# A mixture-of-experts phase in which row indices are listed four blocks ahead and rows gathered three blocks ahead

## The reference

```
scores = sigmoid(xt @ router_w);  sel = scores + router_bias
idx    = top 8 of sel within the best 4 of 8 groups;  wts = scores[idx] / sum * 2.5
# the (token, expert) pairs are sorted by expert and padded to blocks of 128 slots, one expert each
h  = silu(xb @ w1[e]) * (xb @ w3[e])        # xb: 128 gathered rows, w1, w3: 1024 x 256
yb = h @ w2[e]                              # w2: 256 x 1024
out[token] += yb * weight;  out += shared expert
```

## Time and profile before

| | us |
|---|---|
| median of 3 runs | 3874.74 |
| lowest and highest | 3873.43 and 3879.52 |
| span of the profiled execution | 3881.8 |
| from the start of the first scatter to that of the last, layer 0 | 1154.1 to 2146.9 |
| the same, layer 1 | 2901.8 to 3843.6 |

### The profile page before, as it was taken

The page is one execution under the profiler, slowest core; times in us unless marked ns, Lnnn a source line. Parts: engine busy times, 40 slices in busy tenths (PEclk is TensorE's granted clock), DMA queues, the critical chain, the costliest instruction groups (busy, mean ns, idle before and its releaser), DMA issues. The chain is left out here.

```text
span 3881.8 us, 56399 instructions
## 1 busy us (share of the span) xinstructions
PE 3178.2 (82%) x12323; PEld 2159.6 (56%) x12324; DVE 2164.1 (56%) x3866; ACT 1584.7 (41%) x2332; POOL 501.2 (13%) x606
## 2 busy tenths in 40 slices
PE   7988999997768888888888399888668788888884
PEld 1144667763446666666666144454336666666663
DVE  1253433334357767767667520584357777777575
ACT  0033222222136555556555311343135665665564
POOL 0000000000002222222222000000002222222221
PEclk9988555568778898999998699899678988888996
DMA  8721000002059989888888410100348898999796
GB/s 313 251 92 46 1 1 0 1 1 103 37 191 305 301 248 300 289 264 263 255 252 267 161 65 0 46 1 1 118 173 281 286 304 288 300 302 304 226 290 187
DMA packets 156081, 690.47 MB, mean 178 GB/s; under 512 B 15036, under 2 KB 22844, under 8 KB 105044
## 3 DMA queue, kind: packets, MB, share of 16 engines
q1 hardware_dynamic: 111368, 526.73, 36.3%
q0 software_dynamic: 43776, 159.40, 17.7%
q10 hardware_dynamic: 848, 3.24, 0.2%
HBM read 596.95 MB, written 92.37 MB: 178 GB/s over the span
## 5 line engine op out<-in xcount | busy, mean ns | idle before, releaser
L1628 DVE TENSOR_TENSOR e_w13l<-ring,e_w13h x512 | 593.0, 1220 | 67.5 <-issue 44.1
L1536 ACT CAST e_w13h<-ring x512 | 498.1, 1044 | 152.9 <-issue 93.4
L1454 PE MATMUL e_psH<-e_w13h,e_xh 128*128 x1184 | 467.4, 395 | 4.5 <-ACT e_xh L1556 4.0
L1454 PE MATMUL e_psH<-e_w13l,e_xh 128*128 x1184 | 464.1, 392 | 0.0
L1439 PE MATMUL e_psT<-m_id,e_xg 128*128 128x128 f32 x1200 | 209.6, 329 | 260.3 <-DMA e_xg<-h_rows,e_gidx 260.0
L1478 PE MATMUL e_psY<-e_w2h,e_gh 128*128 128x512 f32 x592 | 317.3, 536 | 84.4 <-DVE e_w2l L1615 74.9
L453 PE MATMUL psP<-ring,ho 128*128 128x512 f32 x800 | 350.9, 594 | 0.0
L1393 POOL DMA_INDIRECT y_rows<-e_y,e_sidx x148 | 290.3, 1961 | 369.1 <-ACT e_y L1564 193.8
L1439 PEld LDWEIGHTS e_psT<-m_id,e_xg 128*128 128x128 f32 x1200 | 174.3, 202 | 280.1 <-issue 263.7
L1615 DVE TENSOR_TENSOR e_w2l<-ring,e_w2h 128x1024 fp32r<-128x1024 f32 x256 | 301.2, 1217 | 27.3 <-ACT e_w2h L1525 19.9
L1556 ACT CAST e_xh<-e_psT 128x512 fp32r<-128x512 f32 x300 | 166.5, 588 | 315.3 <-PE e_psT L1439 312.9
(11 more groups left out here) (259 smaller groups left out, 4402.1 us busy)
## 6 DMA issues: line engine op xcount, KB each, us to landing
ring<-in_exp_w SPq DMA_DIRECT2D x388, 1024.0 KB, 5.4
ring<-in_ada_w SPq DMA_DIRECT2D x24, 2048.0 KB, 8.4
ring<-in_c_w_in SPq DMA_DIRECT2D x6, 2048.0 KB, 14.4
bc<-mod_rows SPq DMA_DIRECT2D x4, 1536.0 KB, 8.2
r_bc<-mod_rows SPq DMA_DIRECT2D x4, 1536.0 KB
ring<-in_sh_w SPq DMA_DIRECT2D x6, 1024.0 KB
h_rows<-r_hrow SPq DMA_DIRECT2D x10, 512.0 KB, 2.9
y_rows<-r_y SPq DMA_DIRECT2D x10, 512.0 KB, 2.6
```

The costliest lines, as they stand in the source:

```text
L1454: nc.tensor.matmul(psH[par][:], xh[par][:, k * P:(k + 1) * P], w[:, bass.DynSlice(half, 1), :, k, :], start=(k == 0 and i == 0), stop=False)
L1536: nc.scalar.copy(w13h[:, bass.DynSlice(half, 1), :, k, :].rearrange("p o u k n -> p (o u) (k n)"), raw13[:, bass.DynSlice(half, 1), :, k, ...
L1628: nc.vector.tensor_tensor(low, raw, high.bitcast(F32), ALU.subtract).then_inc(w13_lo, 1)
```

## The change

In experts:

- The row numbers and weights of all blocks go into columns of two tables, e_idxs and e_gws, one column a block. POOL copies a column to e_gidx before a gather and to e_sidx before a scatter; the weight is read by ACT straight from its column.
- choose runs five blocks ahead, index and indices four ahead of the block whose gate is transposed (index(b + 4) and indices(b + 3) in step b), and the gather of b + 5 is issued ahead of scatter(b + 1), so rows are gathered about three blocks ahead. There are still two buffers xg.
- The spare rows move behind the real ones, and an empty slot's row number is T + p (T tokens, p the partition). The gather has a bound: row numbers above T are skipped, and the buffer keeps what was there. xg is cleared once at the start. The scatter still writes all 128 rows.
- PE's order in a step is hidden(b), turn(b + 1), turn_gate(b), index(b + 4), down(b - 1).
- ACT computes SiLU in one instruction instead of the sigmoid, and DVE multiplies once instead of twice.
- ACT's order is silu(b), rows_in(b + 1), gate(b), two of the four pieces of w1 and w3 for b + 2, rows_out(b - 1), split2(b), the other two pieces. DVE's is product(b), indices(b + 3), rows_in(b + 1), gate(b), two pieces, choose(b + 5), rest2(b), the other two pieces.
- The gathers of two blocks behind the last one are gone.

The diff, cut to its core (the starts and ends of the loops and the declarations are left out in part):

```diff
-                link(nc.vector.memset(r.tab5[:, i, :, 3], float((i + 1) * P)))
+                link(nc.vector.memset(r.tab5[:, i, :, 3], float(i * P - T - P)))
             link(nc.vector.tensor_copy(r.tab5[:, :, :, 4], part[:, 0:1].unsqueeze(2).to_broadcast([P, n_t, E])))
-            link(nc.vector.tensor_copy(r.spare[:], part[:, 0:1]))
+            link(nc.vector.tensor_scalar(r.spare[:], part[:, 0:1], float(T), None, ALU.add))
...
+            link(nc.vector.tensor_scalar(r.table[0:1, last + 5:last + 6], r.table[0:1, last + 2:last + 3], 2.0, -4.0, ALU.mult, ALU.add))
...
             def gather(b, par):
-                pool.wait_ge(idx_ready, b + 1)
                 wait_for(pool, xt_mm, 2 * (b - 1))
                 pool.sem_inc(pool_clear, 1)
-                nc.gpsimd.indirect_dma_start(xg[par][:], None, s.hrows[l], bass.IndirectOffsetOnAxis(ap=gidx[par][:, 0:1], axis=0)
-                                             ).then_inc(gathered[par], 16)
+                pool.wait_ge(idx_ready, b + 1)
+                nc.gpsimd.tensor_copy(gidx[par][:], idxs[:, at_block(b)]).then_inc(g_copied, 1)
+                pool.wait_ge(g_copied, b + 1)
+                pool.sem_inc(pool_clear, 1)
+                nc.gpsimd.indirect_dma_start(xg[par][:], None, s.hrows[l], bass.IndirectOffsetOnAxis(ap=gidx[par][:, 0:1], axis=0),
+                                             bounds_check=T, oob_is_err=False).then_inc(gathered[par], 16)
             def scatter(b, par):
-                if isinstance(b, int) and b < 0:
-                    return
-                pool.wait_ge(copied, 2 * b + 2)
+                wait_for(pool, added, 16 * b)
+                pool.sem_inc(pool_clear, 1)
+                nc.gpsimd.tensor_copy(sidx[par][:], idxs[:, at_block(b)]).then_inc(s_copied, 1)
                 pool.wait_ge(y_ready, b + 1)
-                wait_for(pool, added, 16 * b)
+                pool.sem_inc(pool_clear, 1)
+                pool.wait_ge(s_copied, b + 1)
                 pool.sem_inc(pool_clear, 1)
                 nc.gpsimd.indirect_dma_start(s.yrows[l], bass.IndirectOffsetOnAxis(ap=sidx[par][:, 0:1], axis=0), ysb[par][:], None,
                                              compute_op=ALU.add).then_inc(added, 16)
-            def keep(b, par):
-                wait_for(pool, added, 16 * (b - 1))
-                pool.sem_inc(pool_clear, 1)
-                nc.gpsimd.tensor_copy(sidx[par][:], gidx[par][:]).then_inc(copied, 1)
-                nc.gpsimd.tensor_copy(sw[par][:], gw[par][:]).then_inc(copied, 1)
-            def step(b, par):
-                keep(b, par)
-                gather(b + 2, par)
-                scatter(b - 1, 1 - par)
             n = pairs(pool)
+            for par in range(2):
+                nc.gpsimd.memset(xg[par][:], 0.0).then_inc(xg_clean, 1)
+            pool.wait_ge(xg_clean, 2)
...
+            scatter(0, 0)
+            with pool.Fori(0, n - 2) as i:
+                gather(2 * i + 5, 1)
+                scatter(2 * i + 1, 1)
+                gather(2 * i + 6, 0)
+                scatter(2 * i + 2, 0)
...
+            def step(b, m, par):
+                hidden(b, par)
+                turn(b + 1, m, 1 - par)
+                turn_gate(b)
+                index(b + 4, par)
...
-            def pair(i):
-                hidden(2 * i + 1, 1)
-                index(2 * i + 3, 1)
-                turn_gate(2 * i)
-                turn(2 * i + 2, i + 1, 0)
-                down(2 * i, 0)
...
+            step(0, 0, 0)
+            step(1, 1, 1)
+            down(0, 0)
+            with pe.Fori(0, n - 1) as i:
+                step(2 * i + 2, i + 1, 0)
                 down(2 * i + 1, 1)
-            pair(0)
-            with pe.Fori(0, n - 1) as i:
-                pair(i + 1)
-            turn_gate(2 * n)
-            down(2 * n, 0)
+                step(2 * i + 3, i + 2, 1)
+                down(2 * i + 2, 0)
...
-            def expo(b, par):
+            def silu(b, par):
                 act.wait_ge(h_mm, b + 1)
-                wait_for(act, g_step, b)
-                nc.scalar.activation(ge[:], psH[par][:, 0:F], ACT.Sigmoid).then_inc(e_ready, 1)
+                wait_for(act, g_ready, b)
+                nc.scalar.activation(ge[:], psH[par][:, 0:F], ACT.Silu).then_inc(e_ready, 1)
...
-                act.wait_ge(copied, 2 * b + 2)
                 wait_for(act, added, 16 * (b - 1))
-                nc.scalar.activation(ysb[par][:], psY[:], ACT.Copy, scale=sw[par][:, 0:1]).then_inc(y_ready, 1)
+                nc.scalar.activation(ysb[par][:], psY[:], ACT.Copy, scale=gws[:, at_block(b)]).then_inc(y_ready, 1)
             def step(b, par):
-                expo(b, par)
-                gate(b - 1, 1 - par)
+                silu(b, par)
                 rows_in(b + 1, 1 - par)
-                split13(b + 2, range(PIECE))
-                rows_out(b - 1, 1 - par)
+                gate(b, par)
+                split13(b + 2, range(2))
+                if not isinstance(b, int) or b > 0:
+                    rows_out(b - 1, 1 - par)
                 split2(b)
+                split13(b + 2, range(2, PIECE))
...
-            def indices(b, par):
+            def indices(b):
                 dve.wait_ge(idx_mm, b + 1)
-                wait_for(dve, copied, 2 * (b - 1))
-                nc.vector.tensor_reduce(tok[:], psI[:, 3:5], AX.X, ALU.add).then_inc(idx_step, 1)
-                nc.vector.tensor_reduce(gw[par][:], psI[:, 0:3], AX.X, ALU.add).then_inc(idx_step, 1)
-                dve.wait_ge(idx_step, 2 * b + 2)
-                nc.vector.tensor_scalar(gidx[par][:], tok[:], r.spare[:, 0:1], None, ALU.max).then_inc(idx_ready, 1)
+                nc.vector.tensor_reduce(tok[:], psI[:, 3:5], AX.X, ALU.add).then_inc(tok_ready, 1)
+                nc.vector.tensor_reduce(gws[:, at_block(b)], psI[:, 0:3], AX.X, ALU.add)
+                dve.wait_ge(tok_ready, b + 1)
+                nc.vector.tensor_scalar(idxs[:, at_block(b)], tok[:], float(T + P), r.spare[:, 0:1], ALU.add, ALU.min).then_inc(idx_ready, 1)
...
+            def product(b, par):
+                dve.wait_ge(e_ready, b + 1)
+                wait_for(dve, gt_mm, b)
+                nc.vector.tensor_tensor(g[:], ge[:], psH[par][:, F:2 * F], ALU.mult).then_inc(g_ready, 1)
...
-            def silu(b, par):
-                dve.wait_ge(e_ready, b + 1)
-                nc.vector.tensor_tensor(hh[:], ge[:], psH[par][:, 0:F], ALU.mult).then_inc(g_step, 1)
-                dve.wait_ge(g_step, b + 1)
-                wait_for(dve, gt_mm, b)
-                nc.vector.tensor_tensor(g[:], hh[:], psH[par][:, F:2 * F], ALU.mult).then_inc(g_ready, 1)
             def step(b, par):
-                gate(b - 1, 1 - par)
-                indices(b + 2, par)
+                product(b, par)
+                indices(b + 3)
                 rows_in(b + 1, 1 - par)
-                silu(b, par)
-                choose(b + 3, 1 - par)
-                rest13(b + 2, range(PIECE))
+                gate(b, par)
+                rest13(b + 2, range(2))
+                choose(b + 5, 1 - par)
                 rest2(b)
+                rest13(b + 2, range(2, PIECE))
```

More of the change, by code:

```diff
@@ L1304, in experts @@
         sel = [sb(f"e_sel{i}", [P, n_t, P], BF16) for i in range(2)]
+        idxs, gws = sb("e_idxs", [P, P], U32), sb("e_gws", [P, P])
         gidx = [sb(f"e_gidx{i}", [P, 1], U32) for i in range(2)]
-        gw = [sb(f"e_gw{i}", [P, 1]) for i in range(2)]
         sidx = [sb(f"e_sidx{i}", [P, 1], U32) for i in range(2)]
-        sw = [sb(f"e_sw{i}", [P, 1]) for i in range(2)]
         tok = sb("e_tok", [P, 1])
-        ge, hh, g = sb("e_ge", [P, F]), sb("e_hh", [P, F]), sb("e_g", [P, F])
+        ge, g = sb("e_ge", [P, F]), sb("e_g", [P, F])
         gh, gl = ([sb(f"e_g{n}{i}", [P, F], F32R) for i in range(2)] for n in "hl")
@@ L1394, in scatter @@
                                              compute_op=ALU.add).then_inc(added, 16)
-            def keep(b, par):
-                wait_for(pool, added, 16 * (b - 1))
-                pool.sem_inc(pool_clear, 1)
-                nc.gpsimd.tensor_copy(sidx[par][:], gidx[par][:]).then_inc(copied, 1)
-                nc.gpsimd.tensor_copy(sw[par][:], gw[par][:]).then_inc(copied, 1)
-            def step(b, par):
-                keep(b, par)
-                gather(b + 2, par)
-                scatter(b - 1, 1 - par)
             n = pairs(pool)
+            for par in range(2):
+                nc.gpsimd.memset(xg[par][:], 0.0).then_inc(xg_clean, 1)
+            pool.wait_ge(xg_clean, 2)
             gather(0, 0)
             gather(1, 1)
-            step(0, 0)
-            step(1, 1)
-            step(2, 0)
-            with pool.Fori(0, n - 1) as i:
-                step(2 * i + 3, 1)
-                step(2 * i + 4, 0)
-            m = ending(pool)
+            gather(2, 0)
+            gather(3, 1)
+            gather(4, 0)
+            scatter(0, 0)
[4 more added lines that the diff above has]
```

(58 more changed lines are left out.)

42 lines of the change are left out of this document (20 added, 22 removed).

## The result

The changed kernel took 4139.3 us, median of four runs (4137.1 to 4141.7), the kernel before 3877.1 in the same rounds (3873.4 to 3881.4): ratio 1.069, 95% interval 1.067 to 1.071. It is slower by 262 us where 157 us less were forecast. The profiled spans are 4138.1 and 3881.8 us.

A forecast was written before the change was run, and what follows sets the result against it. The index-buffer ring was taken as the bound. Without it, heavy steps of 12.6 us and light ones of 10.8 save 78.5 and 81.4 us in the two layers; with +3.2 that is -156.7, giving 3718 us, range 3645 to 3795.

The forecast's parts named there:

- The ring of before: Index buffer loop through scatter landing, index copy, gather and turn: sets the old step, its removal worth up to 2.2 us.
- The step that failed: PE at turn_gate: waits about 1.5 us for DVE's product in steps that DVE sets, with low clock in part of them.
- a floor of PE: PE's own work per step: 10.2 us, about 12.7 where gate turn, index and down run at low clock.
- a floor of DVE: DVE's own work in a step that brings new weights: 11.9 us.
- ACT: ACT's step: 10.5 us, under DVE's 11.9; only the scatter waits for the eviction of y placed between weight casts.
- Rival D: PE waits at turn_gate keep hidden partly at low clock: step 15 us, +200 us; chance 0.02.
- The DMA floor: DMA service in a step with new weights: between 11.7 and 12.6 us, taken as 12.3, or 12.6 at 98% service.
- rival A: DVE is the only bound, DMA service elastic: heavy steps 11.9 or 12.0 us, time 3620 to 3660; chance 0.14.
- Skipped rows: Empty slots past the gather's bound are free of DMA service: gather loses 0.5 and 0.7 us a step.
- rival B: DMA holds most of the step, skipped rows cost as much as moved: 3788 us, or 3824; chance 0.12.
- Rival C: POOL's chain of scatter, landing and next scatter sets the step: up to 14.2 us, time 4013; chance 0.04.

The follow-up runs named there:

- run 4: Changed kernel with PE, ACT and DVE back in their orders of before; tables, early gather, gather bound and one-instruction SiLU kept: 3560.8 us, 0.920.
- run 9: Variants of run 4: SiLU as sigmoid and multiply 3580.3 us; no gather bound 3542.8; bound on gather and scatter 3527.5; on scatter alone 3528.5.
- run 2: Changed kernel with the four weight pieces together again on ACT and DVE, PE's order as changed: 3968.2 us, 1.024.
- Runs 1 and 5: First: changed kernel with down(b-1) ahead of turn_gate(b), 3778.1 us. Second: run 4 with the change's PE order and choose one block further ahead, 4429.6 us.
- run 6: Changed kernel with PE's register loads for index and down issued ahead of turn_gate's wait: 3840.2 us, 0.991.
- run 7: Changed kernel with 12 idle transposes on PE between turn(b+1) and turn_gate(b), in place of the wait: 3940.3 us, 1.017.

## Why the prediction was wrong

*The ring of before* was read rightly: e_tok's wait and the wait for gathered rows are gone, and run 4, which keeps what removed them, is 314 us faster than before (20 of them SiLU's, by run 9).

*The step that failed* is the one on PE: "When DVE is not free, PE waits for it here: about 1.5 us in a step that DVE sets." and, of the step of 10.2 us that becomes about 12.7 at low clock, "I take it that this happens in part of the steps." The wait was sized about rightly (1.32 and 1.34 us in the steps shown) and the low level of what follows was foreseen, but three things were wrong. It happens in nearly every step (63 waits in 77 steps). The code gaps that I counted on DVE I left out on PE, where there are 1.55 us of them: even with a wait of only 0.21 a PE step took 13.98 us (run 2). And, the step that decided, I set a floor of PE beside a floor of DVE and took the larger; since down(b-1) had been put behind that wait, its time at low clock is handed on to the eviction, the cast, the weight pieces and the next product. The links of a ring add up: 16.0 us in the turn shown and 14.96 on average, not the larger of 11.9 and 12.7. Runs 1 and 5 show it: this one order undone gives back 361 us, and put alone into run 4 it costs 869.

*ACT:* "nothing on the path waits for it except the scatter" failed too. Behind the eviction stands split2, and DVE's e_w2l waits for that (265.5 us in the first phase alone, where the earlier trace rows had 19.9 over the whole span).

*Rival D* had a step of 15 us and +200, near the 14.96 and +262 measured, but by luck: its mechanism is wrong. Hidden is at the high level again, and it is down that runs low. I gave it 0.02 on the ground that after a wait of 2.92 us "products ran at the high level right after", and that was misread. In the kernel before, the turn and then down followed that wait, and down's first eight rows were at the low level:

```profile
3512.14 0.63 PE L1478 MATMUL e_psY<-e_w2l,e_gh 128*128 128x512 f32 x1
...
3514.70 0.63 PE L1478 MATMUL e_psY<-e_w2l,e_gh 128*128 128x512 f32 x1
...
3516.46 0.40 PE L1454 MATMUL e_psH<-e_w13h,e_xh 128*128 x1
```

So down at the low level was there before too (its rows average 536 and 494 ns in that trace); the change made it slow in more steps and put it into the ring.

*The DMA floor* of 12.3 to 13.2 us a step was wrong, though nothing of it shows in the changed kernel. Its upper end came from a stretch with 297 GB/s at a share of 0.94; the same stretch without the ring moved more. The window from 1200 to 1300 us of the variant of 4 with the gather unbound:

```profile
1200.00:1300.00 100.00, 91.81 (x470) 71.79 (x469) 91.38 (x127) 74.69 (x100) 29.65 (x37) 1.00 1.03 378
```

In it the weights moved 28.33 MB in 67.2% of the time and the indirect traffic 9.46 MB in 35.4%. By the prediction's own working that is 7.5 us for an expert in place of 8.77 and 3.9 for a gather and a scatter in place of 4.39. The price of a byte was not fixed, and a share of 94% was no proof of a full resource. Why it differs is not shown. DVE is at 91% in this stretch, which speaks for rival A's bound once the ring is gone, but PE is at 92%, and DMA may still hold part of the steps: in run 4 ACT waits 298.5 us for weights, 59.5 in the kernel before. No run separates them. *Skipped rows* are worth nothing in the gather, where I took 0.5 to 0.7 us a step, which is rival B's premise though not its time: the software queue's bytes fell by a quarter over the span, as forecast (159.40 to 121.69 MB), and no run shows a gain from it.

*Rival C* did not happen in the changed kernel, but its chain comes up where the ring is gone: in run 4 POOL waits 723 us for landings (146 times), and in its first phase the median from issue to landing is 9.6 us against 7.5 in the earlier trace rows. In one step POOL sees the landing, copies and issues the next scatter with no other wait between (scatter at 1505.84, at 1517.90, 12.06 us). Little of this reaches ACT, whose eviction waits 73 us in all for landings. With the scatter's bound these waits are 679 and 55 us; that its 33 us come from there is likely, but not shown.

## What to carry to other kernels

Before an instruction is moved behind a wait on another engine, follow what comes after it through every engine back to that wait; if the way closes, its links add up, and no busy share shows it. Size PE's part of such a ring at the low clock if waits, code gaps and short work stand ahead of it, and put register code ahead of the wait. Try the orders of a change apart from its buffers: here the buffers, with SiLU in one instruction, gave 8% and the orders took 16% (4139 against 3561 us).

## What the runs showed of the hardware

- PE's clock fell to the low level in down after a wait of 1.3 us with gaps of 0.54 and 1.01 us behind it (the changed kernel), after gaps of 0.56 and 0.92 us with no wait in the step shown (run 2), and after a wait of 1.34 us with a gap of 0.24 (run 6). It stayed high over gaps of 0.55 and 0.89 us where 1.47 us of further products stood ahead of them (run 7). The fall can come late: in run 4 a wait of 2.24 us was followed by five rows of 0.49 to 0.39 us, and only then did the rows go to 0.63, from 1524.86 on:

```profile
1523.60 0.49 PE L1467 MATMUL e_psY<-e_w2h,e_gh 128*128 128x512 f32 x1 [2.24 <-ACT e_gh L1536]
...
1524.63 0.39 PE L1467 MATMUL e_psY<-e_w2h,e_gh 128*128 128x512 f32 x1
1524.86 0.55 PE L1467 MATMUL e_psY<-e_w2l,e_gh 128*128 128x512 f32 x1
1525.20 0.63 PE L1467 MATMUL e_psY<-e_w2h,e_gh 128*128 128x512 f32 x1
```

- The core moved 378 GB/s over 100 us in the window of the gather unbound above, with no other core at work for this kernel. The Trainium skill ("SBUF — State Buffer", section "A bandwidth-pool intuition that's wrong") gives about 358 GB/s between HBM and a core; as a ceiling that is not borne out here.
- In run 4 POOL's copy of 128 indices took 0.18 us alone and 1.36 or 1.37 behind a scatter just issued (median 1.36 in that run and 0.18 in the changed kernel, where it does not follow a scatter directly), and each copy was followed by 0.81 to 0.85 us before the transfer that needs it:

```profile
1504.83 0.18 POOL L1376 COPY e_sidx<-e_idxs 128x1 uint32 x1 [5.70 <-DMA y_rows<-e_y,e_sidx]
1505.84 1.75 POOL L1381 DMA_INDIRECT y_rows<-e_y,e_sidx  x1 [0.82 <-POOL e_sidx L1376]
1507.02 1.37 POOL L1366 COPY e_gidx<-e_idxs 128x1 uint32 x1
1509.24 1.18 POOL L1369 DMA_INDIRECT e_xg<-h_rows,e_gidx  x1 [0.85 <-POOL e_gidx L1366]
```
